# Expert blocks of 32 rows in four column tiles, and the first loads of two stages moved a stage ahead, in a hybrid RWKV-7, attention and mixture-of-experts step

## What is computed

```python
xn = _rms_norm(x, lp['norm_mix_g'])
proj = x_cat @ lp['w_in']                     # [r|k|v] of RWKV, [q|k|v] of attention
y_rwkv, s_new = _rwkv7_mix(...)               # recurrence over the tokens, 8 heads of 64
y_att = attn_fn(q, k, v)                      # three dilated windows, 8 heads of 64
h = x + concat(y_rwkv, y_att) @ lp['w_out']
hn = _rms_norm(h, lp['norm_ffn_g'])
h = h + _hier_moe(hn, lp)                     # top-2 of 32 experts inside one group

# inside _hier_moe, for each (token, expert) slot:
(jax.nn.silu(xe @ w1[e]) * (xe @ w3[e])) @ w2[e]     # 1024 -> 512 -> 1024
```

## Time and profile before

| | before |
|---|---|
| median of three runs | 3474.33 us |
| the profiled execution | 3482.01 us, its span 3480.2 us |
| TensorE busy with matmuls | 3171.5 us, 91% |
| VectorE, ScalarE, GpSimd busy | 38%, 29%, 10% |
| granted clock of TensorE, mean | 0.95 |
| moved by DMA | 544.44 MB, mean 156 GB/s |

### The profile page before, as it was taken

One profiled execution on the slowest core, in us unless ns is written; L12 is line 12 of the kernel. 1 busy time (PEld: TensorE's weight loads), 2 busy tenths in 40 slices (PEclk: granted clock), 3 DMA queues, 4 the chain that ended last, 5 costly groups with the idle time before them and its releaser, 6 DMA issues. The chain is left out here.

```text
span 3480.2 us, 75176 instructions
## 1 busy us (share of the span) xinstructions
PE 3171.5 (91%) x31053; PEld 2171.7 (62%) x31054; DVE 1315.8 (38%) x3229; ACT 1014.9 (29%) x2151; POOL 331.2 (10%) x348
## 2 busy tenths in 40 slices
PE   6999999999969888887999979996999999999990
PEld 4667666677738888876877755554555555555550
DVE  3454444554214433433755446664111111111117
ACT  3334433344212222223644453341111111111112
POOL 0000000000010000001433200001110101010104
PEclk9999999999779999998999889997999999999995
DMA  6121111211362332235766546422778686687658
GB/s 207 62 70 64 51 58 51 70 57 49 60 157 100 119 118 89 106 124 174 225 181 183 150 137 213 156 95 95 280 242 285 239 285 234 217 283 242 234 192 303
DMA packets 299222, 544.44 MB, mean 156 GB/s; under 512 B 98338, under 2 KB 122658, under 8 KB 292308
## 3 DMA queue, kind: packets, MB, share of 16 engines
q1 hardware_dynamic: 253180, 401.42, 34.7%
q10 hardware_dynamic: 25000, 66.13, 6.0%
q0 software_dynamic: 20784, 73.15, 5.7%
HBM read 400.66 MB, written 139.98 MB: 155 GB/s over the span
## 5 line engine op out<-in xcount | busy, mean ns | idle before, releaser
L294 PE MATMUL proj_main_ps<-proj_xt,proj_w 128*128 128x257 f32 (+1 forms) x1728 | 391.5, 382 | 0.0
L294 PEld LDWEIGHTS proj_main_ps<-proj_xt,proj_w 128*128 128x128 f32 x1728 | 329.0, 204 | 41.8
L2516 PE MATMUL moe_y_ps<-moe_w,moe_ht 128*64 128x512 f32 x1312 | 301.2, 601 | 3.1 <-ACT moe_ht L2555 3.1
L317 PE MATMUL proj_main_ps<-proj_w,proj_xt 128*128 128x512 f32 (+1 forms) x560 | 248.6, 597 | 0.0
L2264 PE MATMUL out_proj_ps<-out_w,out_ct 128*128 128x512 f32 x544 | 241.5, 597 | 6.2 <-DMA out_w<-in_w_out_dram 6.2
L2566 ACT ACTIVATE moe_sg<-moe_gate 128x256 f32<-128x256 f32 x82 | 31.5, 384 | 535.7 <-PE moe_gate L2500 535.7
L2516 PEld LDWEIGHTS moe_y_ps<-moe_w,moe_ht 128*64 128x64 f32 x1312 | 87.3, 137 | 158.7 <-issue 155.4
L1148 DVE COPY_PREDICATED rwkv_t<-rwkv_cons,rwkv_level_ps 128x512 f32<-128x512 uint32 (+1 forms) x168 | 109.2, 659 | 188.6 <-PE rwkv_level_ps L866 188.4
L317 PEld LDWEIGHTS proj_main_ps<-proj_w,proj_xt 128*128 128x128 f32 (+1 forms) x560 | 102.8, 185 | 124.4 <-issue 122.8
L2264 PEld LDWEIGHTS out_proj_ps<-out_w,out_ct 128*128 128x128 f32 x544 | 101.5, 192 | 122.0 <-issue 121.2
L2602 DVE COPY moe_y<-moe_y_ps 128x512 f32<-128x512 f32 x82 | 56.7, 692 | 313.8 <-PE moe_y_ps L2516 313.8
(11 more groups left out here) (339 smaller groups left out, 5463.3 us busy)
## 6 DMA issues: line engine op xcount, KB each, us to landing
moe_w<-in_expert_w_dram SPq DMA_DIRECT2D x64, 2048.0 KB, 9.7
y_rows<-rwkv_zero POOLq DMA_DIRECT2D x65, 512.0 KB, 4.8
kept_first_gate<-in_expert_w_dram SPq DMA_DIRECT2D x16, 2048.0 KB, 9.8
kept_first_up<-in_expert_w_dram SPq DMA_DIRECT2D x16, 2048.0 KB, 15.1
y_rows<-moe_y ACTq DMA_DIRECT2D x164, 128.0 KB, 6.1
ft_p<-proj_uf SPq DMA_DIRECT2D x32, 642.0 KB, 3.3
rwkv_feat<-ft_p SPq DMA_DIRECT2D x16, 1284.0 KB, 7.1
att_s_k<-in_cache_att_k_dram ACTq DMA_DIRECT2D x14, 1024.0 KB, 6.0
```

The lines of the kernel that those rows point to most:

```text
L294: last = mm(out[:, 0:w + 1], W[:, k, kind * C + m * P:kind * C + (m + 1) * P], XT[n % 2][:, k, 0:w + 1], start=(k == 0), stop=(k == KT - 1))
L317: last = mm(o, x, W[:, k, j * C:(j + 1) * C], start=(k == 0), stop=(k == KT - 1))
L2516: last = mm(py[j * HB:(j + 1) * HB, :], HT[:, c, r * HB:(r + 1) * HB], W2[s][:, k, j * 512:(j + 1) * 512], start=(k == 0), stop=(k == FE / ...
```

## The change

1. **Blocks of 32 rows.** `HB` is 32, and each product is split over four column tiles of 32 columns. The gather reads each token's row as four quarters onto 128 partitions. The counts above make 147 blocks.
2. **Widths.** `X`, `Y` are 256 wide instead of 512, the hidden tiles 128 instead of 256; two X transposes and one hidden transpose for a block instead of four and two. A block is stored with four transfers instead of two.
3. **Index a step ahead.** GpSimd copies the index of block b+3 behind the gather of block b+2, and that copy waits until this gather has landed.
4. **Dispatch.** 197 block columns instead of 132, 32 places instead of 64, four column tiles instead of two.
5. **Sample rows.** The three copies go to three buffers (`O`, `X[1]`, `X[0]`, free by then); the outputs of k and v are stored from ScalarE's queue.
6. **Recurrence's first loads.** The constants and the features of tile 0 are loaded in the projection, before the sample tokens' unit stores.
7. **Attention's first loads.** All four quarters of `QT` are loaded in the recurrence's steps 4 to 7, and three key tiles, identity and mask in step 8.

```diff
-                        if i > 0:
-                            sp.dma_start((kc_s, vc_s)[i - 1][SJ * b:SJ * (b + 1), :], new).then_inc(o_st, 16)
...
                     if n == NP and m == 0:
                         sp.wait_ge(xn_ready, TP + 1)
+                        sp.wait_ge(u_st[0], 32)
+                        sp.wait_ge(u_st[1], 32)
+                        sp.dma_start(next_F[0], ft_p[0]).then_inc(feat_ld[0], 16)
+                        sp.dma_start(next_consts, next_consts_in).then_inc(cons_ld, 16)
...
+            for i in range(1, 3):
+                a.wait_ge(emptied, o_job(NP, i) + 1)
+                for b in range(SB):
+                    nc.scalar.dma_start((kc_s, vc_s)[i - 1][SJ * b:SJ * (b + 1), :], sample_row(i)[SQ1 * b + 1:SQ1 * (b + 1), :]).then_inc(o_st, 16)
...
-                    v.wait_ge(o_st, 32 * TT * NP + (0, 16 * SB, 48 * SB)[i])
-                    v.tensor_copy(O[0:WS, :], main_ps[j % 3][0:WS, :]).then_inc(emptied, 1)
+                    if i == 0:
+                        v.wait_ge(o_st, 32 * TT * NP)
+                    v.tensor_copy(sample_row(i), main_ps[j % 3][0:WS, :]).then_inc(emptied, 1)
...
+                if 4 <= n < 8:
+                    quarter = slice((n - 4) * 4 * P, (n - 3) * 4 * P)
+                    sp.dma_start(next_QT[:, :, quarter], qt[:, :, quarter]).then_inc(next_q_ld[n - 4], 16)
+                if n == 8:
+                    for t in range(len(next_X)):
+                        sp.dma_start(next_X[t][:], k_in[t * P:(t + 1) * P, :]).then_inc(next_x_ld[t], 16)
+                    sp.dma_start(next_ident, ident_in).then_inc(next_c_in, 16)
+                    sp.dma_start(next_mask, mask_in).then_inc(next_c_in, 16)
...
-HB = 64
-NBMAX = 129
+HB = 32
+NQ4 = P // HB
+SHIFT = 5
+NBMAX = 194
...
             def up(bank, W):
                 for k in range(KT):
-                    q, r = k % (KT // 2), k // (KT // 2)
-                    for j in range(2):
+                    q, r = k % KQ, k // KQ
+                    for j in range(NQ4):
                         last = mm(bank[j * HB:(j + 1) * HB, 0:HF], XT[:, q, r * HB:(r + 1) * HB], W[:, k, j * HF:(j + 1) * HF],
                                   start=(k == 0), stop=(k == KT - 1), skip_group_check=True)
...
                 for k in range(FE // P):
-                    c, r = k % 2, k // 2
-                    for j in range(2):
-                        last = mm(py[j * HB:(j + 1) * HB, :], HT[:, c, r * HB:(r + 1) * HB], W2[s][:, k, j * 512:(j + 1) * 512],
+                    for j in range(NQ4):
+                        last = mm(py[j * HB:(j + 1) * HB, 0:DQ], HT[:, k * HB:(k + 1) * HB], W2[s][:, k, j * DQ:(j + 1) * DQ],
...
                 a.wait_ge(y_ev, b + 1)
-                for j in range(2):
-                    nc.scalar.dma_start(y_rows[bass.ds(b * HB - HB, HB), j * 512:(j + 1) * 512], Y[j * HB:(j + 1) * HB, :]).then_inc(y_st, 16)
+                for j in range(NQ4):
+                    nc.scalar.dma_start(y_rows[bass.ds(b * HB - HB, HB), j * DQ:(j + 1) * DQ], Y[j * HB:(j + 1) * HB, :]).then_inc(y_st, 16)
...
+            def index(b):
+                if not start_of_all(b):
+                    g.wait_ge(x_ld, 16 * b)
+                nc.gpsimd.tensor_copy(IX[:], IDX[:, bass.ds(b, 1)]).then_inc(ix_ready, 1)
 
             def load_x(b):
-                nc.gpsimd.tensor_copy(IX[:], IDX[:, bass.ds(b, 1)]).then_inc(ix_ready, 1)
                 g.wait_ge(ix_ready, b + 1)
                 g.sem_inc(go, 1)
-                g.indirect_dma_start(X[:], None, half_rows, bass.IndirectOffsetOnAxis(ap=IX[:], axis=0)).then_inc(x_ld, 16)
+                g.indirect_dma_start(X[:], None, quarter_rows, bass.IndirectOffsetOnAxis(ap=IX[:], axis=0)).then_inc(x_ld, 16)
 
             def step(b, s, i, first):
                 g.wait_ge(x_turned, b + 2)
                 load_x(b + 2)
+                index(b + 3)
```

More of the change, by code:

```diff
@@ L748, in rwkv_chunks @@
         U = ring("u", [P, 5, H, DH], 3)
-        F = ring("feat", [P, 4, FT], 4)
+        F = first_F + [sb(f"feat{j}", [P, 4, FT]) for j in range(1, 4)]
         NB = ring("nt_br", [P, H, P], 3)
@@ L2334, in dispatch_consts @@
     token = np.where(token < prompt + sample, token, 0)
-    half = np.repeat(np.arange(2), HB)[:, None]
+    quarter = np.repeat(np.arange(NQ4), HB)[:, None]
     row = lambda n: np.broadcast_to(np.arange(n), (P, n))
-    return np.ascontiguousarray(np.concatenate([row(HB), row(NBC), 2 * np.repeat(token, 2, 1), half], 1).astype(np.float32))
+    return np.ascontiguousarray(np.concatenate([row(HB), row(NBC), NQ4 * np.repeat(token, 2, 1), quarter], 1).astype(np.float32))
 def dispatch(nc, consts, SLOT, IDX, w1, w3, W1, W3, loaded):
@@ L2349, in dispatch @@
         places, numbers = cn[:, 0:HB], cn[:, HB:HB + NBC]
-        token2, half = cn[:, HB + NBC:HB + NBC + NA], cn[:, HB + NBC + NA:]
+        token4, quarter = cn[:, HB + NBC:HB + NBC + NA], cn[:, HB + NBC + NA:]
         bi = sb("block_int", [P, NA], I32)
@@ L2374, in _ @@
             v.tensor_copy(slot[:], flat)
[L2375 removed]
+            v.tensor_scalar(bi[:], flat, SHIFT, None, ALU.arith_shift_right).then_inc(step, 1)
             v.wait_ge(step, 1)
@@ L2385, in _ @@
             v.wait_ge(listed, 1)
-            v.tensor_scalar(rows[:], table[:, 0:NBC], half, None, ALU.add).then_inc(step, 1)
+            v.tensor_scalar(rows[:], table[:, 0:NBC], quarter, None, ALU.add).then_inc(step, 1)
             v.wait_ge(step, slots_split + 1)
@@ L2478, in _ @@
             end = sp.value_load(BT[0:1, E + 1:E + 2], min_val=2 * E, max_val=NBMAX)
-            sp.wait_ge(y_st, 32 * end + 32)
+            sp.wait_ge(y_st, 64 * end + 64)
             sp.sem_inc(ended, 1)
@@ L2491, in turn_x @@
                     pe.wait_ge(xt_ready, b)
-                for k in range(KT // 2):
+                for k in range(KQ):
                     last = nc.tensor.transpose(px[:, k * P:(k + 1) * P], X[:, k * P:(k + 1) * P], ident[:])
@@ L2505, in turn_hidden_before @@
                 pe.wait_ge(hidden, b)
-                for c in range(2):
-                    last = nc.tensor.transpose(ph[:, c * P:(c + 1) * P], HD[:, c * P:(c + 1) * P], ident[:])
+                last = nc.tensor.transpose(ph[:, 0:P], HD[:], ident[:])
                 last.then_inc(h_turned, 1)
@@ L2590, in step @@
                 load_x(b + 2)
+                index(b + 3)
+            index(0)
             load_x(0)
+            index(1)
             g.wait_ge(x_turned, 1)
             load_x(1)
+            index(2)
             over_experts(g, step)
```

89 lines of the change are left out of this document (43 added, 46 removed).

## The result

The changed kernel takes 3575.28 us (median of four executions, 3554.59 to 3617.02), the kernel before 3473.8 beside it. The ratio is 1.027, 95% interval 1.0214 to 1.0326; it leaves out the longest execution, which has the lowest mean clock (0.934 against 0.945 to 0.952) and is the profiled one, and without it the median is 3567.41, 94 us above the kernel before. The forecast was 3530 with 3440 to 3630, and slower at 0.69. The profiled span is 3615.0 us against 3480.2.

The account below looks back on a forecast made before the run. TensorE's own work was taken to bound the expert stage (busy 947.5 of 950 us). Terms +81 + 1 + 0.5 - 11.5 - 7 - 8 = +56 us gave 3538 profiled, 3530 as median of runs; range 3440 to 3630.

Parts of the forecast that it names:

- TensorE's block: Expert stage: halved products and smaller transposes make a block 6.1 us, 147 blocks 897 us, 54 less than 951.
- rival B: TensorE in expert blocks: weight loads bind at 31.5 ns a pair, 85 us more work, 3565 us in all; chance 0.10.
- The gather: Expert stage: gathers beside weight loads land in 6.1 us and stall TensorE 4.4 us per expert, 135 us in all.
- the third of 0.3: Change of expert: the third gather lands at about 22.9 us, wanted at 22.6, so TensorE stalls 0.3 us.
- Rival A: Expert stage: half-sized gathers hide beside the loads, leaving only ScalarE's 34 us; 45 us faster, 3430 us; chance 0.15.
- The index ahead: GpSimd at a change of expert: the copy waits for the landing, so two block-number reads, 1.8 us, come after it.
- Step 2: Gather needed every 6.1 us: GpSimd's register reads delay the next gather; stalls of 4.4 us per expert, 135 us.
- step 3: ScalarE at a change of expert: stores, then registers, stall TensorE 1.1 us, hidden by the gather's first stall; otherwise 34 us.
- Rival D: Expert stage: clock falls to 1.2 GHz for one block per expert, about 80 us more, 3610 us; chance 0.09.
- Stores: ScalarE's four stores take 2.6 us instead of 1.3, loop 8.6 us beside loads; covered by gather stalls, costed at nothing.
- Dispatch: Dispatch stage: block marks grow by 2.6 us, place marks shrink by about as much; 1 us more, bounds 0 and 3.
- The stage edits: Sample rows, recurrence's and attention's first loads: 11.5, 7 and 8 us less at the stage starts.

Follow-up runs that it names:

- blocks_only: Kernel before with only the 32-row blocks, widths, index ahead and dispatch, without the stage edits: 3562.16 us against 3460.18, ratio 1.0305.
- no_loads: Changed kernel, but from expert 2 on only 8 rows of 64 numbers fetched instead of each 2 MB of weights: 3417.06 us, ratio 0.9868 to the kernel before.
- index_late: Changed kernel with GpSimd copying the index just before each gather, as before the change: 3499.27 us against 3462.85 for the kernel before, ratio 1.0102.
- read_later: Changed kernel reading one block number instead of two before an expert's first block: 3527.83 us against 3476.17 for the kernel before, ratio 1.0154.
- x_staged: Changed kernel with gathers landing in a second buffer, copied to X by GpSimd: 3477.01 us against 3460.18 for the kernel before, ratio 1.0051.
- staged_store: Changed kernel with a second gather buffer and one store per block instead of four: 3615.6 us against 3476.17 for the kernel before, ratio 1.0423.

## Why the prediction was right, and where it was off

It was right in sign, and the range held the time, which came 45 us above the forecast. The expert stage, forecast at 1032 us, took 1093 in the profile after and 1071 in `blocks_only`. By its steps:

1. **TensorE's block.** Forecast 6.1 us and 897 us in all; measured 6.12 and 900. In the gate product the matmuls of the same tile start 109 ns apart, so four tiles make 27 ns a pair. The weight loads hide; rival B (31.5 ns) is out. The Trainium skill, page "TensorE: Matmul & The Clock Gate", section "Part 3: Packing small matmuls", would let weight loads overlap running matmuls only in another row group; with four column tiles that share their rows this trace does not agree, at 27 ns a pair.
2. **The gather.** Right in mechanism (`no_loads`), in place and nearly in size: 135 us forecast, 121 and 102 measured. Its landings of 6.7 and 5.9 us stand beside the 6.1 taken. The stalls of the change shown are 0.6 and 2.4 where 1.3 and 2.8 were forecast, and the third of 0.3 is not there; in `blocks_only` the second is mostly 1.6 to 2.1. The first is smaller because the gate product is itself 1.0 us late. Rival A is out.
3. **The index ahead.** The prediction named its price, the register reads behind the landing, but costed it only through one stall. `index_late` shows some 60 us, since this item lengthens the second stall to where the clock mostly falls behind it.
4. **The register reads on TensorE: the step that failed.** Step 2 counted them on GpSimd and step 3 on ScalarE; TensorE makes the same two, and they had been covered by 3.48 us of down product. With 1.93 us they are not: 22 us that the sum does not have, shown by `read_later`.
5. **The clock.** Rival D, given 0.09, came in part: not a whole block for each expert but 1.7 us behind many of the 2.4 us stalls, 44 us in the profile after and 21 in `blocks_only` (0.02 x 1060). It should have been a term, since the prediction forecast a stall of 2.8 us for each expert and knew that the clock can fall. With 22 and 44 the stage's sum is 897 + 135 + 66 = 1098 for 1093 measured. That it closes so well is partly luck: the gather was taken 14 us too high, and some 11 us of the stage stay unexplained; in `blocks_only`, with 900 of work, 128 idle and 21 of clock, 22 us do.
6. **Stores.** Costed at nothing, and the cover named; right, with VectorE's wait for them at 6.3 us in the profile after. The warning that they would cost without the gather's stalls was right too (`x_staged`).
7. **Dispatch.** From the output projection's first product to the first X transpose are 354.9 us where 352.9 were: 2 us for the 1 forecast. In the ten other profiles with the same dispatch they are 355.7 to 358.2, 2.8 to 5.3 more, nine of them beyond the bound of 3; the last product alone grew from 10.2 us to 13.2 to 14.4.
8. **The stage edits.** The wait between projection and recurrence went from 25.4 us to 9.4, and to 5.8 to 8.9 in the eleven other kernels with the same edits: 16 to 19.6 us for 18.5 forecast. But in `blocks_only`, without these edits, it is 22.1, so some 3 us of that vary by themselves or come with the blocks. In attention 9.84 and 3.50 us of idle time became 5.06 and 0.77: 7.5 for 8. The runs give 12.3 and 21.3 us in all, and the better timed of them (13 to 30) holds the forecast 26.5, the other's (18 less to 9 more) does not. Where the difference goes is open: with the same code the recurrence took 581 and 593 us in two of the kernels, and a drift of that size covers it.

## What to carry to other kernels

A tile made smaller shortens the time that every fixed cost had to hide in: count for each engine what it does once per round or once per outer step (gather, issue, register reads, stores), not only on the engine where it was seen, and compare it with the new period. Stalls on TensorE may cost more than their own length, since the clock can fall behind them; two small edits that kept each stall short gained more time than the waits they removed. When one wait is taken away, look at what it was hiding before counting the gain.

## What the runs showed of the hardware

- Four column tiles of 32 columns with 128 moving columns run at 27 ns a pair and hide their weight loads.
- Behind a stall of 2.43 us the clock granted was 0.57 for the next 2 us, behind another of 2.42 us it stayed at 1.00; behind stalls of 1.14 and 1.68 us in `index_late` the products kept their full pace. The longer the stalls, the more often it fell: during or within 1.5 us behind 1 of 14 stalls of 1.0 to 1.5 us and 10 of 33 of 1.5 to 2.3 in `read_later`, and behind 29 of 31 of 2.3 us or more in `staged_store`.
- A gather of 128 rows of 1 KB lands 2.8 us behind its start alone and 5.6 to 6.8 beside 4 MB of loads in the changes shown, at most 7.5 in the profile after from 2440 to 3330 us. The Trainium skill, page "DMA: Bandwidth & Descriptors", section "Anatomy of one DMA", would make it an estimated 2.3 us; no trace here agrees, the least being 2.6 (`index_late`).
- Beside these loads one store of 128 KB from 128 partitions let the next copy start 9.7 us behind its issue, four of 32 KB, issued one behind the other, after 6.8 (one round of each, in two kernels).
